# Dense expert gates by indirect scatters of single elements instead of one-hot products, in a fused attention and product-key-retrieval layer

## The reference, cut to what matters

```python
s1 = einsum('thd,hkd->thk', q1, keys_a); s2 = einsum('thd,hkd->thk', q2, keys_b)
v1, i1 = top_k(s1, 16);  v2, i2 = top_k(s2, 16)
cand_s = v1[..., :, None] + v2[..., None, :]            # 16 x 16 candidates
cand_i = i1[..., :, None] * 128 + i2[..., None, :]
top_s, pos = top_k(cand_s, 16);  idx = take_along_axis(cand_i, pos)
gates = softmax(top_s)
act = gelu(einsum('td,thkd->thk', h, expert_u[idx]))
y   = einsum('thk,thkd->td', gates * act, expert_v[idx])
```

## Time and profile before

| | |
|---|---|
| median of the runs | 1582.03 us |
| the profiled execution, first to last instruction (its span; the profile lists no other time of its own) | 1579.5 us |
| TensorE busy | 1541.5 us, 98% |
| VectorE busy | 1263.8 us, 80% |
| ScalarE busy | 717.1 us, 45% |
| GpSimd busy | 345.9 us, 22%, 305 instructions |
| DMA | 427.38 MB, mean 271 GB/s |
| mean granted TensorE clock | 0.994 |

### The profile page before, as it was taken

How to read it: one execution, slowest core, us unless ns; L and a number is a source line. 1 busy time by engine, 2 the same in 40 slices (tenths; PEclk the granted TensorE clock), 3 DMA queues, 4 the chain that set the end, 5 groups by cost and what they waited for, 6 DMA issues and landing times.

```text
span 1579.5 us, 23361 instructions
## 1 busy us (share of the span) xinstructions
PE 1541.5 (98%) x8161; PEld 1360.8 (86%) x8161; DVE 1263.8 (80%) x2625; ACT 717.1 (45%) x1128; POOL 345.9 (22%) x305
## 2 busy tenths in 40 slices
PE   6999998999999999999999999999999999999997
PEld 4787666789999999999999999988888888888886
DVE  5775656477988988898999999567888888888886
ACT  4424755353433343343677676434333333333333
POOL 0000002204221222222122222122333333333300
PEclk8999999999999999999999999999999999999999
DMA  8692012046878878789698998999999999999982
GB/s 337 236 359 97 1 66 98 0 170 244 296 245 283 294 235 286 252 276 302 226 320 305 330 322 301 359 333 316 365 347 353 357 350 363 349 358 351 353 285 103
DMA packets 177139, 427.38 MB, mean 271 GB/s; under 512 B 15072, under 2 KB 99200, under 8 KB 172416
## 3 DMA queue, kind: packets, MB, share of 16 engines
q1 hardware_dynamic: 140160, 291.67, 52.7%
q0 software_dynamic: 36864, 134.23, 24.2%
HBM read 373.42 MB, written 52.43 MB: 270 GB/s over the span
## 4 chain that ended last, share of the span: by engine, by line
PE 77%; DVE 1%; issue 1%; ACT 0%; DVEq 0%; ACTq 0%
PE ps_u L1152 11%; PE ps_u L1153 11%; PE ps_u L1154 11%; PE ps_y L1940 11%; PE ps_y L1944 11%; PE ps_y L1942 11%; PE ps_g L1643 5%; PE ps_q L1319 2%; PE ps_q L1321 2%; PE ps_q L1320 2%; PE ps_s L1331 1%; DVE u_lo L1142 0%; PE ps_u L1975 0%; DVE y_scaled L1886 0%; DVE row L1907 0%
## 5 line engine op out<-in xcount | busy, mean ns | idle before, releaser
L1152 PE MATMUL ps_u<-h_hi,u_hi 128*128 128x384 f32 x1024 | 349.0, 341 | 0.3 <-DVE u_lo L1142 0.3
L1154 PE MATMUL ps_u<-h_hi,u_lo 128*128 128x384 f32 x1024 | 344.8, 337 | 0.0
L1153 PE MATMUL ps_u<-h_lo,u_hi 128*128 128x384 f32 x1024 | 344.6, 337 | 0.0
L1811 ACT CAST v_hi<-v_raw 128x1024 fp32r<-128x1024 f32 x128 | 134.7, 1052 | 326.1 <-issue 326.1
L1211 POOL DMA_INDIRECT row<-in_v,row_index x128 | 173.3, 1354 | 375.7 <-DVE h_row L1231 319.4
L1211 POOL DMA_INDIRECT row<-in_u_rows,row_index x128 | 148.2, 1158 | 489.1 <-DVE row_dots L1218 402.2
L1869 DVE TENSOR_TENSOR v_lo<-v_raw,v_hi 128x1024 fp32r<-128x1024 f32 x128 | 160.4, 1253 | 100.4 <-ACT v_hi L1811 99.1
L1940 PE MATMUL ps_y<-v_hi,w_hi 128*128 128x512 f32 x768 | 238.0, 390 | 0.3 <-DVE w_lo L1856 0.3
L1944 PE MATMUL ps_y<-v_hi,w_lo 128*128 128x512 f32 x768 | 237.0, 389 | 0.0
L1942 PE MATMUL ps_y<-v_lo,w_hi 128*128 128x512 f32 x768 | 237.0, 389 | 0.0
L1142 DVE TENSOR_TENSOR u_lo<-u_raw,u_hi 128x1024 fp32r<-128x1024 f32 x128 | 155.0, 1217 | 68.3 <-ACT u_hi L1135 68.3
(11 more groups left out here) (302 smaller groups left out, 2232.8 us busy)
## 6 DMA issues: line engine op xcount, KB each, us to landing
u_raw<-in_u SPq DMA_DIRECT2D x128, 512.0 KB
v_raw<-in_v SPq DMA_DIRECT2D x128, 512.0 KB
activations<-u_act SPq DMA_DIRECT2D x128, 192.0 KB
gate_tiles<-g_tile SPq DMA_DIRECT2D x12, 2048.0 KB
gates<-gate_tiles SPq DMA_DIRECT2D x32, 768.0 KB
act<-activations SPq DMA_DIRECT2D x128, 192.0 KB
w_ada<-in_w_ada SPq DMA_DIRECT2D x23, 1024.0 KB, 7.2
w_proj<-in_w_proj SPq DMA_DIRECT2D x16, 512.0 KB, 4.6
```

Of the source, the lines that this page charges most:

```text
L1152: pe.matmul(out, self.hi[n][:, k], hi, start=(k == 0), stop=False)
L1153: pe.matmul(out, self.hi[n][:, k], lo, start=False, stop=False)
L1154: last = pe.matmul(out, self.lo[n][:, k], hi, start=False, stop=(k == KD - 1))
```

## The change

`dense_gates` goes, with its PSUM banks, one-hot tiles and tile stores. In its place:

- a DRAM tensor of 16384 x 384 single elements is zeroed by six stores of 4.2 MB from one zeroed 4 KB row a partition, issued by SP in the stick-breaking stage, and waited for by SP at the end of the next stage;
- in turn h + 1 VectorE works out for head g = h: the cells (expert x 384 + token), and, for picks that an earlier head already has, the sum of those earlier gates (compare, multiply, reduce over 16 x 16g pairs, for two token tiles and then one), and adds it to the own gate;
- GpSimd scatters these values, one indirect DMA of 128 elements for each of 3 token tiles and 16 picks, 48 a head. A head's first scatter waits for its values and for all scatters of the head before to have landed. Row gathers stand between the scatters;
- the last head's values come in the nine steps from U block 78 on; turns 6 and 7 have 11 U blocks each;
- dots are fewer in the turns (30 instead of 81 by their end); the rest are spread over U blocks 87 to 127 and V blocks 0 to 13. The gelu of the rows moves to V block 14, the adds are spread over V blocks 16 to 122;
- SP waits for all scatters at U block 120 and then issues the first V loads; U blocks 78 to 127 are all in `experts`; gates are loaded in runs of 384 elements.

```diff
+FILLS = 6
-G_TOK = 32
-G_TILES = DENSE // G_TOK
+SPREADS = DENSE_TILES * TOPK
-TURN_START = [0, 6, 16, 26, 36, 46, 56, 66, 80]
-DOTS_BY = [0, 0, 8, 20, 32, 44, 56, 68, 81]
-GATED = 120
+TURN_START = [0, 6, 16, 26, 36, 46, 56, 67, 78]
+DOTS_BY = [0, 0, 8, 14, 19, 23, 26, 28, 30]
+GATED = TURN_START[PEER_HEADS]
+LATE_GATHERS, LATE_STEPS = 24, 9
...
 def stick_breaking(...):
...
+            sp.wait_ge(blank_done, 1)
+            for n in range(FILLS):
+                sp.dma_start(flat[:, n * part:(n + 1) * part].rearrange("p (a n) -> p a n", n=D),
+                             blank[:].rearrange("p (o n) -> p o n", o=1).broadcast_to([P, part // D, D])).then_inc(keep["filled"], 16)
...
 def retrieval(...):
...
-            for h in range(PEER_HEADS):
-                for r in range(gathered(h), gathered(h + 1)):
-                    rows.gather(pool, r)
+            for r in range(rows.RING):
+                rows.gather(pool, r)
+            for g in range(PEER_HEADS):
+                for n in range(SPREADS):
+                    spread_gate(pool, g, n)
+                    for r in gathers_at(g, n):
+                        rows.gather(pool, r)
+
+        def spread_gate(pool, g, n):
+            b, j = n // TOPK, g * TOPK + n % TOPK
+            if n == 0:
+                pool.wait_ge(summed, g + 1)
+                if g > 0:
+                    pool.wait_ge(spread, 16 * SPREADS * g)
+            pool.indirect_dma_start(out=g_dram, out_offset=bass.IndirectOffsetOnAxis(ap=cell[:, b, j:j + 1], axis=0),
+                                    in_=owed[:, b, j:j + 1], in_offset=None).then_inc(spread, 16)
+
+        def gathers_at(g, n):
+            done = lambda g: DOTS_BY[g + 2] if g + 2 <= PEER_HEADS else DOTS_BY[PEER_HEADS] + LATE_GATHERS * (g + 2 - PEER_HEADS)
+            first, last = rows.RING + done(g - 1), rows.RING + done(g)
+            return range(first + (last - first) * n // SPREADS, first + (last - first) * (n + 1) // SPREADS)
...
                 settle(0.3)
                 dve.sem_inc(s_read, 1)
+                g = h - 1
+                if g >= 0:
+                    gates_of(dve, g)
+                    note(cells_of(dve, g))
...
+                if g > 0:
+                    note(equal_picks(dve, g, 0, 2))
...
                 settle(0.46)
+                if g == 0:
+                    dve.sem_inc(summed, 1)
+                if g > 0:
+                    note(equal_gates(dve, g, 0, 2))
...
                 settle(0.8)
                 dve.sem_inc(e_in, 1)
+                if g > 0:
+                    dve.sem_inc(summed, 1)
...
+        def equal_picks(dve, g, b, n):
+            mine = expert[:, b:b + n, own(g)].rearrange("p b (k o) -> p b k o", o=1).broadcast_to([P, n, TOPK, g * TOPK])
+            return dve.tensor_tensor(twin(g, n), mine, earlier(expert, g, b, n), ALU.is_equal)
+
+        def equal_gates(dve, g, b, n):
+            return dve.tensor_tensor(twin(g, n), twin(g, n), earlier(gate, g, b + 1, n), ALU.mult)
+
+        def equal_sums(dve, g, b, n):
+            return dve.tensor_reduce(twins[:, b:b + n], twin(g, n), AX.X, ALU.add)
...
 def experts(...):
...
-        FIRST_ADD = 2 - OPENING
+        LAST_DOT, FIRST_ADD, LAST_ADD = 14, 16, N_KEYS - 5
+        LOADS_AT = -8
...
+        def dots_at(i):
+            had, span = DOTS_BY[PEER_HEADS], LAST_DOT + OPENING - LATE_STEPS
+            by = lambda i: had + (PICKS - had) * min(span, max(0, i + OPENING - LATE_STEPS)) // span
+            return range(by(i), by(i + 1))
...
             for i in range(-OPENING, N_KEYS):
+                if i == LOADS_AT:
+                    sp.wait_ge(spread, 16 * SPREADS * PEER_HEADS)
+                    load_gates(0)
...
         def gpsimd(pool):
-            for r in range(PICKS + rows.RING, ROWS):
+            for r in range(rows.RING + DOTS_BY[PEER_HEADS] + LATE_GATHERS, ROWS):
                 rows.gather(pool, r)
...
                 if i < 0:
                     up.vector_at(dve, N_KEYS + i)
-                if i == 1 - OPENING:
+                if i + OPENING < LATE_STEPS:
+                    first["late_gates"](dve, i + OPENING)
+                for r in dots_at(i):
+                    rows.dot(dve, r, h_row)
+                if i == FIRST_ADD - 1:
                     dve.wait_ge(rows.acted, 1)
```

More of the change, by code:

```diff
@@ L786, in _ @@
             sp.dma_start(keep["w_out"][:], io["w_out"]).then_inc(keep["w_out_in"], 16)
+            sp.wait_ge(keep["filled"], 16 * FILLS)
         @block.gpsimd
@@ new lines, in late_gates @@
+        def late_gates(dve, n):
+            link = lambda ins: ins.then_inc(late, 1)
+            dve.wait_ge(late, n)
+            if n == 0:
+                gates_of(dve, LAST)
+                link(cells_of(dve, LAST))
+            elif n < 7:
+                b, tiles = (0, 2) if n < 4 else (2, 1)
+                part = (equal_picks, equal_gates, equal_sums)[(n - 1) % 3]
+                link(part(dve, LAST, b, tiles))
+            elif n == 7:
+                link(owe(dve, LAST))
+            else:
+                dve.tensor_copy(rows.gate[:], gate[:, 0])
+                dve.sem_inc(summed, 1)
@@ L1705, in experts, with owe @@
+        def owe(dve, g):
+            return dve.tensor_tensor(owed[:, :, own(g)], gate[:, 1:TB, own(g)], twins[:], ALU.add)
+        return {"late_gates": late_gates, "sync": sync, "gpsimd": gpsimd, "tensor": tensor, "scalar": scalar, "vector": vector}
+def experts(nc, life, io, keep, up, rows, h_row, g_dram, spread, first):
     with ExitStack() as ctx:
@@ L2037, in program @@
             fsb = lambda n, s, d=F32: front.enter_context(nc.sbuf_tensor(n, s, d))
-            picks = (fsb("expert", [P, TB, P]), fsb("gate", [P, TB, P]))
-            first = retrieval(nc, top, io, keep, picks, up, rows, h_row, query)
+            first = retrieval(nc, top, front, io, keep, up, rows, h_row, query, g_dram, spread)
             query_banks.close()
-            second = dense_gates(nc, top, keep, picks, up, rows, h_row, g_dram, g_stored)
-        third = experts(nc, top, io, keep, up, rows, h_row, g_dram, g_stored)
+        second = experts(nc, top, io, keep, up, rows, h_row, g_dram, spread, first)
         block = top.enter_context(nc.Block())
@@ L2046, in _ @@
         def _(sp):
-            for stage in (first, second, third):
+            for stage in (first, second):
                 stage["sync"](sp)
```

268 lines of the change are left out of this document (73 added, 195 removed).

## The result

The changed kernel takes 1729.27 us, the median of 4 runs (1723.85 to 1738.77), beside 1582.62 for the kernel before on the same chip: a ratio of 1.0937, with a 95% interval from 1.0921 to 1.0953. It is slower. The forecast was 1688 and slower. A second job ran the same file at 1728.31. The profiled execution has a span of 1737.0 us; it is the slowest of the four. The profile of the second job, with a span of 1727.0 us, is nearer the medians, and is given beside it where the two differ.

A forecast was written before the change was run, and what follows sets the result against it. TensorE bound the kernel before; GpSimd's queue would after. Span = E + 93.8 + 537.7 + 5 = 1046.5 + 438c, 1686 us at c = 1.46; median 1688. Range 1497 to 1755, the forecast's own 1592 to 1755.

The forecast's parts named there:

- The mechanism: GpSimd's issue queue makes rows late, so VectorE's dots, then TensorE wait; V starts near 1143 us; chance 0.58.
- The cost of one issue: GpSimd's time per scatter or gather with its gap: taken as 1.46 us, between under 0.94 and 1.74.
- E: Time when head 7's last scatter and gather are done on GpSimd: 392 + 438c + 18, 1050 us at 1.46.
- c: Cost of one GpSimd issue in us, taken as 1.46; the span meets the old 1579.5 at 1.22.
- The sums: VectorE's added operations for repeated picks: 73 us in all, 15.7 in turn 7, covered; 0, at most 5.
- The path behind E: From E to V's start: landing 4, dot 1.2, u_lo 1.2, 21 blocks 87.4; in sum 93.8 us.
- V's stage: From V's start to the end: 537.7 us as before, plus 5 for late dots' transfers; denser adds 0.
- The zeros: Six stores, 25 MB, issued between 150.2 and 229.2 us, take 62 to 71 us, ending before the load at 229.2.
- The turns: Turn 7 holds 51 us of VectorE work in 45.8 of TensorE's, covered; unhindered, block 78 starts at 743.0.
- A cheap issue: First rival: a scatter costs 0.7 to 1.1 us with its gap; time 1496 to 1531; chance 0.34.
- The DMA engines' burden: Second rival: 49,152 single elements load the DMA engines, 97 us late, about 1593 even with cheap issues; chance 0.05.
- the size of the prize: 90.8 us leave TensorE with the one-hot stage; if nothing waits, V starts at 951.0, unhindered time 1494.

The follow-up runs named there:

- the run with late loads: Changed kernel with V's first ten loads issued at U block 126 in place of 120: 1770.99 us in a disturbed job, 1725.36 us when run again.

## Why the prediction was right, step by step

**The mechanism** held at each link that was named: GpSimd without a break from 392 to past 1000, but for the waits for landings that the sum has; starts 1.27 us apart at least (forecast 1.24); dots that wait over 100 us (265.7); TensorE late for u_lo from block 91 on, which is at 822.5, at the lower clock; V late, at 1191.4 and not near 1143. The kernels without scatters, with three quarters of them and with memsets in their place show that the cause is the queue and its length: whatever moved the queue's end, between 938.5 and 1072.6, V started 117 to 120 us behind it in all five undisturbed profiles with 288 or 384 scatters, or memsets, and V's loads at block 120.

The size was short: 41 us in the median (1688 against 1729.27), 51 in the profile taken apart here.

**The cost of one issue.** E came at 1072.6, in place of 1050 at c = 1.46. Of the 680.4 us from 392.2, some 9 went into waits for landings (18 forecast), and 672 / 437 makes c = 1.54; in the second profile E is 1061.3 and c 1.51. The mean gather of the earlier trace rows was measured where the queue mostly waited; issues without a break, over VectorE's turns at 1.60 and over its idle time at 1.27, come out between. The sums, which the forecast priced on VectorE at nothing, are the difference by way of GpSimd: that step asked who is behind them on VectorE and not whom they lock out. Without them c is 1.44. So 1.46 fits a queue without the sums, and that it came so near there is luck: it was the mean of another queue.

**The path behind E** was the term that was mis-sized most: 118.8 us, not 93.8. Block 107 starts at 1080.8, E + 8.2 (forecast 6.4); the 21 blocks from there take 110.6 us, not 87.4, and 95.9 in the run with late loads. "SP issues its V loads at block 120 ... and the queued u loads behind it, cost nothing" failed: 12 us by the run with late loads. SP's queue in the changed kernel:

```profile
1142.89 3.85 SPq L1694 DMA_DIRECT2D v_raw<-in_v  x2
1146.78 2.09 SPq L1706 DMA_DIRECT2D act<-activations  x2
1148.92 4.32 SPq L1700 DMA_DIRECT2D gates<-dense_gates  x1
1153.28 7.24 SPq L1139 DMA_DIRECT2D u_raw<-in_u  x1
```

An issue of 0.33 us took 7.24. The stores of the activations stand behind these loads, ScalarE waits for a store before it may reuse its buffer, TensorE for ScalarE. The cover that the forecast named, 54 us between E and the loads, was there in time but not in transfers: once the rows came free, they and the blocks held the DMA engines (0.95 over the whole stretch). The other 13 us were not taken apart; with late loads TensorE's granted clock is still 0.96 over the 21 blocks.

**V's stage** took 545.6 us, against 537.7 + 5. The denser adds and the late dots were hidden, at 371 GB/s and a share of 1.00: more than the 354 that the earlier trace rows shows, as was assumed. **The zeros** landed in 33.0 us each in the median, ahead of the load at 229 us, and delayed nothing. **The turns** cost TensorE 3.7 us of waits, and block 78 started at 753.1 in place of 743.0 (at 746.6 to 749.0 in six other profiles, that without scatters among them); GpSimd's queue hid it.

Together: 1686 + 23 + 25 + 3 = 1737, the profiled span.

**The rivals.** A cheap issue is out: the shortest of the 384 took 0.965 us. The DMA engines' burden is out as the main cause, since memsets of a like length, with no transfer, lose too, and the rest is the longer issues; at a share of 0.13 in the hole there was room. What the rival of the cheap issue had right is the size of the prize: without scatters 1512.

## What to carry to other kernels

Count an engine's queue in issues and not in busy time. GpSimd was busy 61.5 of 287.7 us, and yet 48 more issues a turn were 77 us in a turn of 54.4; 16 more fitted, with even blocks, and won 0.65%. Here an indirect DMA of 128 indices held the queue as long for single elements as for whole rows of 4 KB, and VectorE operations put beside the full queue, hidden on VectorE, were paid on GpSimd: 33 us. Look at what a late queue releases when it catches up: what was spread over 300 us comes at once.

## What the runs showed of the hardware

- One indirect DMA on GpSimd: 0.97 us for 128 elements of 4 bytes, 0.94 to 0.99 for 128 rows of 4 KB, each with 0.30 us between; up to 6.94 us under two-input operations of VectorE, 1.23 and 1.19 in the mean of 384 in two profiles. The Trainium skill (DMA: Bandwidth & Descriptors, "Latency and other measured facts") puts the first byte of this path at about 1 us, for the work of writing descriptors. When the first byte moves no run here shows; that the queue is held 0.97 us, the trace does.
- A head's 48 scatters had landed at the latest 1.9 to 4.8 us after the last of their issues ended, seven times: with one gather between, the next head's first scatter started then.
- The DMA engines moved 402 to 416 GB/s in single stretches at a share of 1.02 and 1.03; just behind such a stretch of the changed kernel an issue on SP took 7.24 us.
- In one job of five, TensorE and the others crept for tens of us at a time in programs with scatters, with no wait named, while the kernel before, in the same job, took its 1582. It was gone in a later job on another chip. What it is was not found.
